# Spreading a token tile's gates over 16 slots of one chunk, with selection over 12 slots, in a two-layer expert network kernel

## What is computed

```python
q = (x @ w_pq).reshape(bsz, seq, PEER_HEADS, 2, PEER_KEY_DIM)
scores = jnp.einsum('bshcd,hcnd->bshcn', q, sub_keys)
top_v, top_i = lax.top_k(scores, PEER_TOPK)                # 16 of 128, for 8 heads x 2 halves
cand = top_v[..., 0, :, None] + top_v[..., 1, None, :]
best_v, best_pos = lax.top_k(cand, PEER_TOPK)              # 16 of the 256 pairs
idx = jnp.take_along_axis(cand_idx, best_pos, axis=-1)     # expert = first * 128 + second
gate = jax.nn.softmax(best_v, axis=-1)
...
h = jax.nn.gelu(jnp.einsum('ted,td->te', expert_u[it], xt))
return jnp.einsum('te,ted->td', gt * h, expert_v[it])
```

## Time and profile before

| | us |
|---|---|
| median of 3 runs | 3925.08 |
| lowest and highest | 3922.57, 3931.66 |
| the profiled execution, its own time | 3924.02 |
| its span | 3922.3 |
| TensorE busy | 3442.4 (88%) |
| VectorE busy | 2989.1 (76%) |
| ScalarE busy | 1478.1 (38%) |
| GpSimd busy | 1093.0 (28%) |

### The profile page before, as it was taken

One profiled execution on the slowest core, in us unless ns is written; L12 is line 12 of the kernel. 1 busy time (PEld: TensorE's weight loads), 2 busy tenths in 40 slices (PEclk: granted clock), 3 DMA queues, 4 the chain that ended last, 5 costly groups with the idle time before them and its releaser, 6 DMA issues.

```text
span 3922.3 us, 57979 instructions
## 1 busy us (share of the span) xinstructions
PE 3442.4 (88%) x19870; PEld 1971.8 (50%) x19870; DVE 2989.1 (76%) x5160; ACT 1478.1 (38%) x1972; POOL 1093.0 (28%) x748
## 2 busy tenths in 40 slices
PE   7778987988887889999886889879888888899997
PEld 3334643555454546666542346435454545566664
DVE  5887535798888868888848865358989897688887
ACT  4314432335353533333342144233353535333333
POOL 1640000041313224444326300001413131344443
PEclk9889998999999999999998899999999999999998
DMA  4000312486969599999640003124869696999995
GB/s 170 22 0 11 129 49 86 143 281 220 327 210 334 204 374 371 371 389 372 232 136 12 0 22 129 43 94 166 289 227 318 222 319 215 382 370 375 386 367 199
DMA packets 385870, 840.08 MB, mean 214 GB/s; under 512 B 32576, under 2 KB 231232, under 8 KB 384960
## 3 DMA queue, kind: packets, MB, share of 16 engines
q1 hardware_dynamic: 311424, 564.60, 40.9%
q0 software_dynamic: 73728, 268.47, 18.5%
q10 hardware_dynamic: 576, 5.37, 0.3%
HBM read 731.36 MB, written 106.95 MB: 214 GB/s over the span
## 4 chain that ended last, share of the span: by engine, by line
PE 28%; DVE 11%; issue 3%; DMA 3%; ACT 2%; SPq 2%; POOL 1%; DVEq 0%; ACTq 0%; POOLq 0%
PE ps L1582 4%; PE ps L1584 4%; PE ps L1583 4%; PE ps L116 3%; PE ps L118 3%; PE ps L117 3%; DVE wl L95 2%; DMA wf<-experts 2%; DVE xT L1741 1%; SPq L82 1%; PE ps L592 1%; DMA xT<-urows,small 1%; ACT wh L89 1%; PE ps L152 1%; DVE small L1706 0%
## 5 line engine op out<-in xcount | busy, mean ns | idle before, releaser
L116 PE MATMUL ps<-xh,wh 128*128 128x384 f16 (+1 forms) x2880 | 1004.8, 349 | 211.3 <-DVE wl L95 63.4
L95 DVE SCALAR_TENSOR_TENSOR wl<-wf,wh 128x1024 f16<-128x1024 f32 x656 | 804.2, 1227 | 435.3 <-ACT wh L89 420.5
L89 ACT ACTIVATE wh<-wf 128x1024 f16<-128x1024 f32 x656 | 690.9, 1054 | 1042.2 <-PE ps L1584 591.7
L117 PE MATMUL ps<-xl,wh 128*128 128x384 f16 (+1 forms) x2880 | 1002.8, 348 | 0.0
L118 PE MATMUL ps<-xh,wl 128*128 128x384 f16 (+1 forms) x2880 | 1001.4, 348 | 0.0
L1681 POOL DMA_INDIRECT xT<-urows,small x256 | 363.1, 1418 | 1168.5 <-DVE xT L1741 883.8
L1582 PE MATMUL ps<-work,wh 128*128 128x384 f16 x2048 | 667.7, 326 | 6.9 <-DVE work L1866 5.1
L1584 PE MATMUL ps<-work,wl 128*128 128x384 f16 x2048 | 667.6, 326 | 0.0
L1583 PE MATMUL ps<-work,wh 128*128 128x384 f16 x2048 | 667.6, 326 | 0.0
L1689 POOL DMA_INDIRECT work<-experts,small x256 | 448.7, 1753 | 583.4 <-DVE work L1875 558.0
L116 PEld LDWEIGHTS ps<-xh,wh 128*128 128x128 f16 x2880 | 286.9, 100 | 473.2 <-ACT work L1624 102.4
(11 more groups left out here) (334 smaller groups left out, 4317.1 us busy)
## 6 DMA issues: line engine op xcount, KB each, us to landing
wf<-experts SPq DMA_DIRECT2D x512, 512.0 KB, 5.7
wf<-proj SPq DMA_DIRECT2D x144, 512.0 KB, 3.3
gates<-work SPq DMA_DIRECT2D x48, 1024.0 KB, 10.4
work<-hid SPq DMA_DIRECT2D x256, 192.0 KB, 4.4
work<-gates SPq DMA_DIRECT2D x256, 192.0 KB, 5.3
hid<-work SPq DMA_DIRECT2D x192, 192.0 KB, 6.0
hid<-small SPq DMA_DIRECT2D x64, 192.0 KB, 5.4
xsave<-xT ACTq DMA_DIRECT2D x2, 2048.0 KB, 6.9
```

The lines of the kernel that those rows point to most:

```text
L89: m.nc.scalar.activation(m.wh[:, slot, :], m.wf[:, k, :], ACT.Copy, scale=WS).then_inc(m.high_done, 1)
L95: m.nc.vector.scalar_tensor_tensor(m.wl[:, slot, :], m.wf[:, k, :], WS, m.wh[:, slot, :], ALU.mult, ALU.subtract).then_inc(m.split_done, 1)
L116: m.nc.tensor.matmul(out, wh[:, k, :], xh[:, k, 0:n], start=(k == order[0]), stop=False)
L117: m.nc.tensor.matmul(out, wh[:, k, :], xl[:, k, 0:n], start=False, stop=False)
```

## The change

R_SEL goes from 5 to 3 and R_CHUNK from 2 to 4, so that a token tile has 12 selection slots and 16 spread slots of one chunk each (CPH = 1); R_TOK stays 9 and no stage boundary between token tiles moves. STORES goes from 8 to 16, of 512 KB each: one a slot for token tiles 1 and 2, two a slot for tile 3. The dots get a new rule: at most 1.0 us of room in the slots in which stores run (`storing`), at most 1.9 elsewhere. With the new numbers the spread slots have room for dots.

```diff
--- before.py
+++ after.py
@@ -1340,14 +1340,14 @@
 TO = TC // TI
 CPT = P // TC
 R_PQ = N_PQ // RING
-R_SEL = 5
-R_CHUNK = 2
+R_SEL = 3
+R_CHUNK = 4
 R_PICK = 1
 R_TOK = R_SEL + 2 + R_CHUNK
 R_U = EB // RING
 ST_N = NT - 1
 R_LAST = R_U - R_PICK - ST_N * R_TOK
-STORES = 8
+STORES = 16
 TURN = RING - 1
 AHEAD = RING - 1
 ND = SEQ - P
@@ -1381,9 +1381,15 @@
     return 1.3 + CPH * 2.8
 
 
+def storing(j):
+
+    at = j - R_PICK * RING
+    return at >= R_TOK * RING and at % (R_TOK * RING) < STORES
+
+
 def dots_by(j):
 
-    room = [min(1.8, max(0.0, 5.6 - other_work(i))) for i in range(EB)]
+    room = [min(1.0 if storing(i) else 1.9, max(0.0, 5.6 - other_work(i))) for i in range(EB)]
     return int(sum(room[:j]) * N_SEL / sum(room) + 0.5)
 
 
@@ -1462,12 +1468,14 @@
             sp.wait_ge(m.tile_out, N_PQ + j + 1 + 2)
             sp.dma_start(m.hid[j], gst[j % RING]).then_inc(m.g_out[j % RING], 16)
             for tt in range(1, NT):
-                c = j - spread_slots(tt).stop
-                if c in range(STORES):
-                    i = slice(c * EB // STORES, (c + 1) * EB // STORES)
+                at, per = j - spread_slots(tt).stop, 2 if tt == NT - 1 else 1
+                if at == 0:
                     sp.wait_ge(m.staged, tt * CPT + 2)
-                    sp.dma_start(m.gates[i, :, (tt - 1) * P:tt * P].rearrange("i j t -> j i t"), stage[:, i, :])\
-                        .then_inc(m.gates_out, 16)
+                for c in range(at * per, at * per + per):
+                    if c in range(STORES):
+                        i = slice(c * EB // STORES, (c + 1) * EB // STORES)
+                        sp.dma_start(m.gates[i, :, (tt - 1) * P:tt * P].rearrange("i j t -> j i t"),
+                                     stage[:, i, :]).then_inc(m.gates_out, 16)
 
         for j in range(EB):
             if j >= LATER:
```

## The result

The changed kernel takes 3955.07 us (median of four runs, 3949.55 to 3959.84) against 3923.86 us (also four runs): ratio 1.0076, 95% interval 1.006 to 1.0093, slower by more than the noise. The prediction was 3947 us, range 3908 to 3975, slower with a chance of 0.65. The profiled execution, the slowest of the four, took 3959.84 us with a span of 3958.1 us, 35.8 more than before's span. In the new file lines from about 1390 on have moved: the gelu is L1632, a dot L1749, a chunk's last operation L1840, its matmuls L1572.

A forecast was written before the change was run, and what follows sets the result against it. VectorE was taken as the bound, except where stores load the DMA engines, with VectorE and TensorE waiting in turns in the spread. Layer 1 +10.2 and layer 2 +11.5 gave +21.7 on the profiled execution: 3947 us, range 3908 to 3975.

The forecast's parts named there:

- Selection: The 12 selection slots: VectorE stays the bound and costs its sum, 68.3, 64.8 and 64.9 us for tiles 1 to 3.
- list of signs: Expected trace marks, among them VectorE over 95% busy in selection, ScalarE load waits near zero, spread slots averaging 5.9 us.
- price of `choose`: VectorE in selection: 1.69 us for an even half, 3.70 for an odd half, 43.1 us a stage.
- the 8 us of idle time: VectorE's idle during selection's 1 MB stores, counted as gone for tiles 2 and 3 with 512 KB stores.
- the walk with 9.27 us: Pick and turn: four row buffers, 9.27 us gather round trip; dots wait 4.4 us in tile 1, 3.4 in tiles 2, 3.
- 1.59 - x: Spread: if TensorE waited x before a chunk, it waits 1.59 - x before the next, 2.74 - x after two dots.
- Tile 1 and the tail: Layer 1: tile 1 takes 209.8 us, +19.4; the stage after slot 112 gains 8.4 us from six fewer gathers.
- (a): Spread: pairing of VectorE and TensorE isn't binding, slots cost VectorE's sum of 4.99 us, total 3869; chance 0.12.
- (b): Pick and turn: gather round trip falls under 7.5 us and waits vanish, 11.2 us a layer, total 3925; chance 0.16.
- (c): Selection and tail: stores still hold up loads, 8 us for tiles 2 and 3, tail gains nothing, total 3996; chance 0.07.
- (d): Spread: each gather's issue on GpSimd, about 1 us, holds up the chunk operation beside it, +120, total 4067; chance 0.03.
- (e): Tail freed by 15 us, double dots where TensorE is late anyway (-1 a tile), (b) in part, total 3913; chance 0.07.

The follow-up runs named there:

- e4: Kernel before with only the stages changed (12 selection slots, 16 spread slots of one chunk), old 1 MB stores and old dot rule: 3944.7 us, ratio 1.0044.
- e10: Changed kernel with each chunk built one slot early and eight 1 MB stores again, same dots: 3861.2 us, ratio 0.9839.
- e5: Changed kernel with the old rule for dots (at most 1.8 us of room in every slot): 3948.8 us, ratio 1.006.
- e7: Changed kernel with room for only one dot in each spread slot, but for one slot: 3962.5 us, ratio 1.0096.
- e2: Changed kernel with VectorE building each chunk one slot early, order otherwise the same: 3863.1 us, ratio 0.9837.
- e3: Kernel before with only the stores changed, to 16 of 512 KB, stages and dots as before: 3891.6 us, ratio 0.9906.
- e6: e3 with later chunks built one place earlier, still two chunks a slot over 8 spread slots: 3885.5 us, ratio 0.9903.

## Why the prediction was right

The prediction said +21.7 us in the profiled execution; it was +35.8. By medians it was +31.2 where the forecast is +23.1. The direction, the mechanism and the bounds held; what follows goes term by term through the profiled execution, the only one with a trace and the slowest of the four.

**Selection.** By sums 68.3 us for tile 1; VectorE took 68.6 (767.4 to 835.9). Tile 2: 64.8 against 65.1 (977.7 to 1042.8). The waits view of the changed kernel in this stretch:

```profile
ACT wh L89 <- DMA wf<-experts: 2.0, 2, 1.4
...
DVE wl L95 <- ACT wh L89: 2.6, 1, 2.6
```

ScalarE's load waits, 38.1 us before, are 2.0. VectorE is busy in 92% of the stage by the windows view and not in over 95%, as the prediction's list of signs has it: its sums go from start to start, and the view leaves out the gaps between operations. The price of `choose` held, and so did the step that the 8 us of idle time go. It credited them to the wrong cause, though: the stores were also spread out, but e4 and e10 show that the longer slots alone, 5.4 us of VectorE's work, do it. That part came right with a reason that wasn't needed. Nor was 388 GB/s, as the prediction has it, a mix of much smaller transfers than 1 MB: the stretch is the one in which the 1 MB stores run.

**Pick and turn.** Tile 2's dots waited for their gathers 3.4 us in three places, as the walk with 9.27 us gave. VectorE's timeline, changed kernel:

```profile
1042.82 0.29 DVE L1796 TENSOR_TENSOR rs<-small 128x128 f32<-128x128 f32 x1
...
1070.93 1.23 DVE L1749 SCALAR_TENSOR_TENSOR xT<-xT,work 128x1024 f32<-128x1024 f32 x1 [0.95 <-DMA xT<-urows,small]
...
1073.81 1.23 DVE L1749 SCALAR_TENSOR_TENSOR xT<-xT,work 128x1024 f32<-128x1024 f32 x1 [0.18 <-DMA xT<-urows,small]
...
1077.31 1.23 DVE L1749 SCALAR_TENSOR_TENSOR xT<-xT,work 128x1024 f32<-128x1024 f32 x1 [2.27 <-DMA xT<-urows,small]
```

**The spread.** The rule "1.59 - x", worked out with the plan of dots, gives slots of 4.9, 6.5, 6.1, 5.4, 6.1, 5.4, 7.2, 4.9, ... for tile 1; the marks read 4.9, 6.6, 6.1, 5.4, 6.1, 5.4, 7.3, 4.9. The mean slot is 6.0, 6.2 and 6.0 us in the three tiles where the prediction has 5.9. The forecast for tile 1 missed at one slot of the fifteen, which took 8.9 us instead of 7.2.

**The term that was mis-sized** is what follows a slot with two dots. The prediction had TensorE wait up to 2.7 us there and go on at full speed. Timelines of VectorE and TensorE, changed kernel, slots 61 to 63:

```profile
1089.60 1.23 DVE L95 SCALAR_TENSOR_TENSOR wl<-wf,wh 128x1024 f16<-128x1024 f32 x1 [3.95 <-ACT wh L89]
...
1090.74 1.22 DVE L1749 SCALAR_TENSOR_TENSOR xT<-xT,work 128x1024 f32<-128x1024 f32 x1
...
1091.89 1.22 DVE L1749 SCALAR_TENSOR_TENSOR xT<-xT,work 128x1024 f32<-128x1024 f32 x1
...
1094.87 0.68 DVE L1840 TENSOR_TENSOR sq<-work,rs 128x1024 f16<-128x1024 f16 x1
...
1095.61 0.33 PE L1572 MATMUL ps<-work,sq 128*128 128x128 f16 x1 [2.60 <-DVE sq L1840]
...
1097.33 0.52 PE L116 MATMUL ps<-xh,wh 128*128 128x384 f16 x1
...
1099.13 0.33 PE L116 MATMUL ps<-xh,wh 128*128 128x384 f16 x1
...
1102.06 0.22 PE L1572 MATMUL ps<-work,sq 128*128 128x128 f16 x1
```

Split, two dots and the chunk end at 1095.5; TensorE has waited 2.60 us, and the matmuls after it take 0.52 us until 1099.1, when they are back at 0.33. The granted clock over these 3.5 us is 0.51 and 1.00 behind them, the levels of 1.2 and 2.4 GHz, and the slot takes 9.2 us instead of 7.7. Of the twelve spread slots in both layers with such a wait (2.1 to 2.6 us), eight ran 1.4 to 1.8 us over the rule and four did not, one of them with a wait of 2.58 us. Together that is 13 of the 14 us that the sum lacked. e4, e5 and e7, whose longest wait behind chunk 0 is 1.4 to 1.5 us in all spreads, have no such slot.

**Tile 1 and the tail.** Tile 1 is 21.7 us longer against the 19.4 of the sum, 1.7 of the difference being the clock. From slot 112 to the end of the layer -8.9 and -6.1 against -8.4 each; of that, the slots 112 to 127 themselves give -8.1 and -7.7.

**The rivals.** (a), slots at the sum of 4.99, was refused by the order in which VectorE works, as the prediction argued, and e2 is that rival made true: 3863 against its 3869. (b): the waits for gathers didn't vanish; VectorE waited 10.6 us for them in layer 1's tiles against 11.2 in the sum. (c): the waits of ScalarE went. (d): all 256 dots and the chunk operations kept their durations (the 310 chunk operations that run beside a gather's issue take 0.686 us on average, the 82 others 0.684), so the gathers beside them cost nothing that the trace shows. The exclusive lock of the port pair that the Trainium skill describes ("SBUF — State Buffer", the section on the two sides of SBUF) doesn't show in these rows. (e): the tail gave 8 us and not 15, and the slots with two dots cost time instead of none.

**Where the change's gain went.** Its three parts are not worth what they are worth alone. The stores alone give 35 us (e3). The stages alone cost 18 (e4). e4's spread of 86.5 us is 12.8 over the 15 x 4.91 that TensorE's own work takes; before's 44.3 is 2.9 over 7 x 5.92. These 10 us more are the pairing of VectorE and TensorE. In tiles 2 and 3 selection over 12 slots gives back nearly as much, in tile 1, where no store runs beside it, almost nothing. The stages also make the stores' gain vanish, since selection isn't held up by late loads in the first place (e5, e10). The rule for dots adds about 6, at the edge of noise.

## What to carry to other kernels

Where two engines hand work to each other each round, add up not only each engine's work but the loop: what stands in the consumer's order between the event that releases it and the piece that its partner waits for. Here 4.9 and 5.0 us of work made slots of 6.0 to 6.2 (5.8 in e4 and e5), and building the piece one round early took all of that away for a change of two lines. It took away little where a round held two pieces and the sum of one engine was already near the round's length (e6). And before spreading transfers out, look at how long the engine behind the loads stops: neither the sum of the load waits (38.1 us before, 43.8 in the faster e3) nor the longest of them (7.1 before, 6.8 in e10, where VectorE stopped for 2.5 us in all) tells the cost.

## What the runs showed of the hardware that was not expected

TensorE's granted clock fell to the 1.2 GHz level behind single waits for VectorE in a stage in which TensorE was otherwise busy: the matmuls at 1097.33 are at 0.52 us after the wait of 2.60 us, those from 1099.13 on at 0.33 again. With eight of the twelve waits of 2.1 to 2.6 us in the changed kernel's spreads the slot was longer by 1.4 to 1.8 us, with four it wasn't; what tells them apart stays open. The spreads of e4, e5 and e7, whose longest wait was 1.4 to 1.5 us, have no such slot. Stores of 512 KB over 16 slots in place of 1 MB over eight shortened the longest wait of a load from 7.1 to 4.3 us while the sum of the waits rose from 38.1 to 43.8.
